# Keys and inputs of a recurrent head transposed as row tiles in one group, attention one weight tile earlier, and two multiplications on VectorE instead of GpSimd

## The reference, cut to what matters

```python
h = rmsnorm(x, w_norm_pre)
proj = h @ w_in                      # q_a k_a v_a z_a (attention), q_r f_r i_r z_r (recurrence)
# attention: 8 query heads, 2 key heads, chunks of 64 tokens; a chunk sees itself and the one before
s = q_a . k_a * 64 ** -0.5
p = softmax([s, sink])[..., :-1]     # one sink logit a head
o_a = (p @ v_a) * silu(z_a)
# recurrence: 4 heads of width 128
f = lb + (1 - lb) * sigmoid(f_r);  kk = 1 - f
G = cumsum(log f)                    # within a chunk
A = tril((q_r * exp(G)) @ (kk * exp(-G)).T)
o = A @ i_r + (q_r * exp(G)) @ S_prev      # S_prev: state carried from chunk to chunk
U = (kk * exp(G_last - G)).T @ i_r;  S = exp(G_last) * S_prev + U
o_r = rmsnorm(o, hgrn_norm) * silu(z_r)
y = [o_a, o_r] @ w_out
out = x + rmsnorm(y, w_norm_post)
```

## Time and profile before

| | |
|---|---|
| median of 3 runs | 909.15 us (907.79 to 909.39) |
| the profiled execution | 906.35 us |
| its span in the trace | 904.4 us |
| TensorE (PE) busy | 884.2 us, 98% |
| TensorE weight loads (PEld) busy | 725.4 us, 80% |
| VectorE (DVE) busy | 520.0 us, 58% |
| ScalarE (ACT) busy | 423.7 us, 47% |
| GpSimd (POOL) busy | 167.6 us, 19% |
| share of PE in the chain that ended last | 86% |
| granted TensorE clock, mean | 0.997 |

### The profile page before, as it was taken

One profiled execution on the slowest core, in us unless ns is written; L12 is line 12 of the kernel. 1 busy time (PEld: TensorE's weight loads), 2 busy tenths in 40 slices (PEclk: granted clock), 3 DMA queues, 4 the chain that ended last, 5 costly groups with the idle time before them and its releaser, 6 DMA issues.

```text
span 904.4 us, 12126 instructions
## 1 busy us (share of the span) xinstructions
PE 884.2 (98%) x4616; PEld 725.4 (80%) x4616; DVE 520.0 (58%) x829; ACT 423.7 (47%) x750; POOL 167.6 (19%) x122
## 2 busy tenths in 40 slices
PE   7998989989999999999999999999999999999997
PEld 6786867878888787888888878888888887888886
DVE  6758877675553765655244577555515366744523
ACT  7756365564355534544234444454423443445322
POOL 0001232430200023242020021353002001213102
PEclk9999999999999999999999999999999999999999
DMA  8686664747967842543676652444378553335463
GB/s 308 234 295 203 206 204 154 278 150 266 419 215 270 278 175 98 184 165 141 243 283 234 226 213 106 148 174 167 115 298 325 190 177 116 139 137 179 140 238 135
DMA packets 52633, 186.01 MB, mean 206 GB/s; under 512 B 5856, under 2 KB 6112, under 8 KB 52576
## 3 DMA queue, kind: packets, MB, share of 16 engines
q1 hardware_dynamic: 49840, 178.29, 55.5%
q10 hardware_dynamic: 2736, 6.95, 1.9%
HBM read 141.18 MB, written 44.04 MB: 205 GB/s over the span
## 4 chain that ended last, share of the span: by engine, by line
PE 86%; DVE 6%; issue 4%; ACT 2%; POOL 2%; DMA 1%; SPq 0%; DVEq 0%; ACTq 0%; POOLq 0%
PE bank L428 54%; PE bank L437 10%; PE turn_b L437 5%; PE score_b L437 5%; PE turn_b L476 2%; PE score_b L454 2%; PE bank L508 1%; PE bank L524 1%; PE bank L515 1%; PE bank L522 1%; PE bank L493 1%; DVE w_lo L865 1%; PE bank L501 1%; DMA w_raw<-in_weights 1%; PE turn_b L466 1%
## 5 line engine op out<-in xcount | busy, mean ns | idle before, releaser
L428 PE MATMUL bank<-h_hi,w_lo 128*128 128x512 f32 x832 | 329.2, 396 | 0.7 <-DVE w_lo L877 0.7
L428 PE MATMUL bank<-h_lo,w_hi 128*128 128x512 f32 x832 | 329.0, 395 | 0.0
L428 PE MATMUL bank<-h_hi,w_hi 128*128 128x512 f32 x832 | 327.5, 395 | 1.4 <-issue 0.6
L428 PEld LDWEIGHTS bank<-h_lo,w_hi 128*128 128x128 f32 x832 | 156.7, 188 | 36.7 <-issue 6.4
L428 PEld LDWEIGHTS bank<-h_hi,w_hi 128*128 128x128 f32 x832 | 156.7, 188 | 35.1 <-issue 2.7
L428 PEld LDWEIGHTS bank<-h_hi,w_lo 128*128 128x128 f32 x832 | 156.7, 188 | 33.8 <-DVE w_lo L877 1.4
L1135 POOL TENSOR_TENSOR probs<-probs,s_stats 128x1024 f32<-128x1024 f32 x16 | 33.1, 2067 | 349.6 <-DVE s_stats L1007 349.6
L865 DVE TENSOR_TENSOR w_lo<-w_raw,w_hi 128x1024 fp32r<-128x1024 f32 x37 | 47.2, 1282 | 33.0 <-ACT w_hi L656 33.0
L660 ACT ACTIVATE g_a<-g_b 128x512 f32<-128x512 f32 x32 | 20.2, 632 | 89.8 <-DVE g_b L929 89.8
L933 DVE SCALAR_TENSOR_TENSOR g_a<-g_b,g_a 128x512 f32<-128x512 f32 x32 | 35.3, 1102 | 44.2 <-ACT g_a L662 44.2
L1163 POOL TENSOR_TENSOR mix_lo<-v_r,mix_hi 128x512 fp32r<-128x512 f32 x16 | 20.7, 1294 | 169.9 <-ACT v_r L798 169.9
(11 more groups left out here) (161 smaller groups left out, 1439.6 us busy)
## 6 DMA issues: line engine op xcount, KB each, us to landing
w_hi<-kept_hi SPq DMA_DIRECT2D x96, 512.0 KB, 3.7
w_lo<-kept_lo SPq DMA_DIRECT2D x96, 512.0 KB, 4.7
w_raw<-in_weights SPq DMA_DIRECT2D x40, 512.0 KB, 5.5
kept_hi<-w_hi SPq DMA_DIRECT2D x34, 512.0 KB, 5.7
kept_lo<-w_lo SPq DMA_DIRECT2D x34, 512.0 KB, 7.2
x_in<-in_x_rows SPq DMA_DIRECT2D x8, 1024.0 KB, 7.2
x_in<-in_x SPq DMA_DIRECT2D x15, 512.0 KB, 6.8
out<-q_gate ACTq DMA_DIRECT2D x9, 512.0 KB, 9.4
```

The costliest lines, as they stand in the source:

```text
L428: mm = pe.matmul(acc(w)[:, :], stationary[:, s, k, :], moving[:, k, :], start=(m == 0), stop=(m == 3 * KT - 1), skip_group_check=True)
```

## The change

1. `SCORES0` goes from `Z0 + 3` to `Z0 + 2`: every quarter of attention is one weight tile earlier (scores at `w` = 8, 10, 12, 14). `weigh` moves from m = 17 to m = 20. The offsets of `MIXA` grow by one, so that those copies stay at steps 20 and 21.
2. `turn_keys` and `turn_inputs` go. `head_scores` (now `gate(h)`, m = 12) transposes both as 16 transposes of 64 partitions in two row groups, into the two banks of `score_b`; then, without waiting for a copy, it makes the scores in `head_b`. ScalarE copies both with one instruction of 128x1024 instead of two of 128x512. `head_states`, `scores(3)` and the start of the output projection wait for that copy (`kv_ready`).
3. `head_out` moves from m = 12 to m = 8, `head_sum` from m = 20 to m = 18, and it writes `score_b[:, 1, :]`. It no longer waits for `o_gated`; the scores of the next head do.
4. The normalisation of `probs` moves from GpSimd to the end of `softmax_sums` on VectorE, the product `k_mid` from GpSimd to VectorE, ahead of the scaling of `f_d`.

```diff
-SCORES0 = Z0 + 3
+SCORES0 = Z0 + 2
-MIXA = {SCORES0 + CHUNKS + 3: (0, 1), SCORES0 + CHUNKS + 4: (2, 3)}
+MIXA = {SCORES0 + CHUNKS + 4: (0, 1), SCORES0 + CHUNKS + 5: (2, 3)}
...
 # scores(t, q)
+                for h in range(HEADS):
+                    if gate(h) + 1 == SCORES0 + 2 * q:
+                        pe.wait_ge(kv_ready.sem, kv_ready.after(t, h))
...
-            def turn_keys(t, h):
+            def head_scores(t, h):
                 pe.wait_ge(k_mid_done.sem, k_mid_done.after(t, h))
+                pe.wait_ge(tile_read.sem, tile_read.after(t, value(h)))
+                pe.wait_ge(m_sub.sem, m_sub.after(t, PAIRS - 1 if gate(h) >= SCORES0 + CHUNKS else (gate(h) - SCORES0) // 2))
                 pe.wait_ge(o_rstd.sem, o_rstd.after(t, h - 1))
-                for p in range(PAIRS):
-                    mm = pe.transpose(head_b[:, pair(p)], k_mid[:, pair(p)], ident)
-                mm.then_inc(k_turned.sem, 1)
...
+                for a, src in enumerate((k_mid, v_r)):
+                    for p in range(PAIRS):
+                        for j in range(2):
+                            half = slice(64 * j, 64 * j + 64)
+                            mm = pe.transpose(score_b[:, j, chunk(PAIRS * a + p)], src[half, pair(p)], ident[half, half])
+                mm.then_inc(kv_turned.sem, 1)
+                pe.wait_ge(o_gated.sem, o_gated.after(t, h - 1))
                 for p in range(PAIRS):
                     mm = pe.matmul(head_b[:, pair(p)], k_mid[:, pair(p)], q_mid[:, pair(p)], start=True, stop=True)
                 mm.then_inc(a_done.sem, 1)
...
 # head_sum(t, h)
                 pe.wait_ge(o_low.sem, o_low.after(t, h))
-                pe.wait_ge(o_gated.sem, o_gated.after(t, h))
-                pe.matmul(head_b[:, :], ones_r[:, :], o_sq_hi, ...)
+                pe.matmul(score_b[:, 1, :], ones_r[:, :], o_sq_hi, ...)
...
 # between(t, w, m)
-                    if w == gate(h) and m == 4:
-                        turn_keys(t, h)
-                    if w == gate(h) and m == 10:
-                        turn_inputs(t, h)
-                    if w == gate(h) and m == 17:
+                    if w == gate(h) and m == 12:
                         head_scores(t, h)
-                    if w == gate(h) + 2 and m == 12:
+                    if w == gate(h) + 2 and m == 8:
                         head_out(t, h)
-                    if w == gate(h) + 3 and m == 20:
+                    if w == gate(h) + 3 and m == 18:
                         head_sum(t, h)
-                if m == 17 and not odd and 1 <= q <= PAIRS:
+                if m == 20 and not odd and 1 <= q <= PAIRS:
                     weigh(t, q - 1)
...
 # scalar, at s == gate(head), now behind the copy of turn_b
+                            act.wait_ge(kv_turned.sem, kv_turned.after(t, head))
+                            act.activation(kv_tok[:, :, :].rearrange("p a (b j n) -> p j (a b) n", j=2, n=CHUNK),
+                                           score_b[:, :, :].rearrange("p j (b n) -> p j b n", n=CHUNK), ACT.Copy).then_inc(kv_ready.sem, 1)
...
 # vector, softmax_sums(t, q)
-                dve.reciprocal(s_inv[:, :], s_sum[:, :]).then_inc(p_inv.sem, 1)
+                then(t, dve.reciprocal(s_inv[:, :], s_sum[:, :]))
+                dve.tensor_tensor(probs[:, :, :], probs[:, :, :], s_inv[:, :].unsqueeze(2).broadcast_to([P, 8, P]),
+                                  ALU.mult).then_inc(p_normed.sem, 1)
...
 # vector, kind 1 (step forget(h) + 2)
                         dve.wait_ge(f_exp.sem, f_exp.after(t, h_of))
+                        dve.wait_ge(a_done.sem, a_done.after(t, h_of - 1))
+                        dve.tensor_tensor(k_mid[:, :], f_a[:, :], f_b[:, :], ALU.mult).then_inc(k_mid_done.sem, 1)
                         dve.tensor_tensor(f_d[:, :], f_d[:, :], x_scale[:, :], ALU.mult).then_inc(f_d_scaled.sem, 1)
```

More of the change, by code:

```diff
@@ L234, in hybrid_block @@
         scored, turned, weighed = (count(n, PAIRS) for n in ("scored", "turned", "weighed"))
-        k_turned, v_turned, a_done, u_done = (count(n, HEADS) for n in ("k_turned", "v_turned", "a_done", "u_done"))
+        kv_turned, a_done, u_done = (count(n, HEADS) for n in ("kv_turned", "a_done", "u_done"))
         o_done, o_summed = count("o_done", HEADS), count("o_summed", HEADS)
@@ L241, in hybrid_block @@
         p_exp, p_turned, v_win_ready = count("p_exp", PAIRS), count("p_turned", PAIRS), count("v_win_ready", 1)
-        k_ready, v_ready, o_squared, o_rstd = (count(n, HEADS) for n in ("k_ready", "v_ready", "o_squared", "o_rstd"))
+        kv_ready, o_squared, o_rstd = (count(n, HEADS) for n in ("kv_ready", "o_squared", "o_rstd"))
         mixa_hi, mixh_hi = count("mixa_hi", QT), count("mixh_hi", HEADS)
@@ L252, in hybrid_block @@
         a_masked, state_done, o_gated, head_mixed = (count(n, HEADS) for n in ("a_masked", "state_done", "o_gated", "head_mixed"))
-        m_sub, p_inv, gated = (count(n, PAIRS) for n in ("m_sub", "p_inv", "gated"))
+        m_sub, gated = (count(n, PAIRS) for n in ("m_sub", "gated"))
         h_lo_done = count("h_lo_done", KT)
@@ L257, in hybrid_block @@
         y_read, y_biased, finished = count("y_read", 8), count("y_biased", 1), count("finished", 8 - len(Y_POOL))
-        dve_step = count("dve_step", 1 + len(ROPE_TILES) + PAIRS * 4 + HEADS * 8)
+        dve_step = count("dve_step", 1 + len(ROPE_TILES) + PAIRS * 5 + HEADS * 8)
         dve_setup, lb_step = sem("dve_setup"), sem("lb_step")
@@ L413, in _ @@
         def _(pe):
-            for c in (tile_done, x_summed, y_done, values_turned, scored, turned, weighed, k_turned, v_turned, a_done, u_done, o_done, o_summed):
+            for c in (tile_done, x_summed, y_done, values_turned, scored, turned, weighed, kv_turned, a_done, u_done, o_done, o_summed):
                 c.start(pe)
@@ L530, in head_sum @@
                 pe.wait_ge(o_low.sem, o_low.after(t, h))
-                pe.wait_ge(o_gated.sem, o_gated.after(t, h))
-                pe.matmul(head_b[:, :], ones_r[:, :], o_sq_hi, start=True, stop=False, skip_group_check=True)
-                pe.matmul(head_b[:, :], ones_r[:, :], o_sq_lo, start=False, stop=True,
+                pe.matmul(score_b[:, 1, :], ones_r[:, :], o_sq_hi, start=True, stop=False, skip_group_check=True)
+                pe.matmul(score_b[:, 1, :], ones_r[:, :], o_sq_lo, start=False, stop=True,
                           skip_group_check=True).then_inc(o_summed.sem, 1)
@@ L596, in _ @@
                 pe.wait_ge(mixa_lo.sem, mixa_lo.after(t, QT - 1))
+                pe.wait_ge(kv_ready.sem, kv_ready.after(t, HEADS - 1))
                 order = [(2 * w + i, b) for w in range(3) for b in range(4) for i in range(2)] + [(KT - 2, b) for b in range(4)]
@@ L635, in _ @@
         def _(act):
-            for c in (hi_split, swapped, gate_ln, gate_sig, f_ln, f_sig, f_log, f_exp, p_exp, p_turned, v_win_ready, k_ready, v_ready,
+            for c in (hi_split, swapped, gate_ln, gate_sig, f_ln, f_sig, f_log, f_exp, p_exp, p_turned, v_win_ready, kv_ready,
                       o_squared, o_rstd, mixa_hi, mixh_hi, x_squared, h_hi_done, y_squared, x_rstd, y_rstd, act_step):
@@ L759, in _ @@
                         gate_first(t, QT + h)
-                    for head in range(HEADS):
-                        if s == gate(head):
-                            act.wait_ge(k_turned.sem, k_turned.after(t, head))
-                            act.activation(kv_tok[:, 0, :], head_b[:, :], ACT.Copy).then_inc(k_ready.sem, 1)
                     if not odd and 1 <= q <= PAIRS:
@@ L800, in _ @@
                             act.wait_ge(o_summed.sem, o_summed.after(t, head))
-                            rstd(t, head_b[:, :], o_scale[:, :], P).then_inc(o_rstd.sem, 1)
+                            rstd(t, score_b[:, 1, :], o_scale[:, :], P).then_inc(o_rstd.sem, 1)
                     if s == V_TURN + 1:
@@ L1121, in _ @@
         def _(pool):
-            for c in (lo_split, k_mid_done, o_low, p_normed, mixa_lo, mixh_lo, x_added,
+            for c in (lo_split, o_low, mixa_lo, mixh_lo, x_added,
                       y_scaled, finished_pool):
@@ L1131, in split_lo @@
                 pool.tensor_tensor(w_lo[:, s, :, :], w_raw[:, i % RAW_SLOTS, :, :], w_hi[:, s, :, :], ALU.subtract).then_inc(lo_split.sem, 1)
-            def norm_probs(t, q):
-                pool.wait_ge(p_inv.sem, p_inv.after(t, q))
-                pool.tensor_tensor(probs[:, :, :], probs[:, :, :], s_inv[:, :].unsqueeze(2).broadcast_to([P, 8, P]),
-                                   ALU.mult).then_inc(p_normed.sem, 1)
             def add_x(tile, k):
@@ L1167, in _ @@
                                                ALU.subtract).then_inc(mixh_lo.sem, 1)
-                    if odd and 0 <= q < PAIRS:
-                        norm_probs(t, q)
                     for i in splits(t, s):
@@ L1172, in _ @@
                             split_lo(i)
-                    if kind == 1:
```

(3 more changed lines are left out.)

13 lines of the change are left out of this document (1 added, 12 removed).

## The result

The changed kernel takes 900.17 us, the median of four runs (899.35 to 901.49). The kernel before, timed beside it, takes 908.47 us, the median of four (906.3 to 909.39). The ratio is 0.9915, with a 95% interval of 0.9896 to 0.9934. The forecast was 900.8 us, in a range of 895.5 to 907.2.

A forecast was written before the change was run, and what follows sets the result against it. Matmul time was taken to bound token tiles 2 to 4, with VectorE's and ScalarE's pace also counting in the first. Gains of 6.9 + 1.5 = 8.4 us gave 900.8 us by the median, range 895.5 to 907.2.

The forecast's parts named there:

- The walk: First token tile, engine lists laid side by side: PE enters the output projection 6.9 us sooner; counting waits gave 5.7.
- The refund: First tile, VectorE: seven instructions stretched by GpSimd's two products give back 8 us together, against 7.2 added.
- The waits left: First tile, PE: waits remaining after the change sum to 6.5 us, against 11.7 lost before.
- the slack: `weigh(1)`: a wait of about 1.0 us in the first tile; 0.5 us to spare in token tiles 2 to 4.
- PE's own saving: Every tile: merged row-tiled transposes save 0.12 us a head, 0.5 a token tile, 2.0 over four.
- so 0.78 without them: PE: 16 row-tiled transposes cost 0.78 us, from 1.23 with four keys' transposes behind them.
- all waits of the first tile would go: Rival, first tile: 11.7 + 2.0 = 13.7 us gained, 895.5 us; chance 0.14.
- VectorE's pace would be no better: Rival, first tile: waits only change place, PE's own time alone is saved, 907.1 us; chance 0.16.
- the clock falls at the new wait: Rival, first tile: behind `head_scores(3)`'s wait of 2.8 us the slow clock takes 1.6 us, 902.4 us; chance 0.09.
- VectorE's list as the bound: Rival, first tile: the added 7.2 us come on VectorE's path without refund, 914.4 us; chance 0.09.
- no wait in token tiles 2 to 4: Later token tiles: PE still never waits, so 3 x 0.5 = 1.5 us gained.
- the loop: First tile, behind `v_r`: PE transposes, ScalarE copies and makes `mix_hi` and `w_hi`, then VectorE splits; a head still takes 29.8 us.

The follow-up runs named there:

- without part 4: Changed kernel with normalisation and `k_mid` back on GpSimd, all else as changed: 903.82 us, ratio 0.9954 to the kernel before.
- the split ahead of the copy: Changed kernel, with ScalarE making `w_hi` at gate steps ahead of its wait for the turned keys and values: 896.4 us, ratio 0.9875 to the kernel before.
- part 4 alone: Kernel before with only normalisation and `k_mid` moved from GpSimd to VectorE: 904.83 us, ratio 0.9964.
- two changes of order on ScalarE and GpSimd: Changed kernel with `w_hi` ahead of the wait for turned keys and values, and `MIXA`'s second pair at step 22 instead of 21: 894.63 us, ratio 0.9848.
- attention late: Changed kernel with attention back at its old weight tiles (scores at 9, 11, 13, 15), all else as changed: 910.74 us, ratio 1.0023 to the kernel before.
- Attention sooner alone: Kernel before with attention one weight tile sooner, `weigh` still at m = 17, both products on GpSimd: 907.73 us, ratio 0.9994.
- parts 1 and 4: Kernel before with attention one weight tile sooner, `weigh` at m = 17, and normalisation and `k_mid` on VectorE: 901.31 us, ratio 0.9929.
- with `head_sum` waiting: Changed kernel with `head_sum` waiting for `o_gated` again: 903.19 us, ratio 0.9939 to the kernel before.

## Why the prediction came out right, and where its sum was wrong

**The place.** PE's waits in the first token tile were to shrink, and they did. Idle time of PE there went from 10.1 to 4.4 us. `forget(2)` starts at 140.07; 139.5 was expected, and this profile began `w` = 8 some 1.3 us later than that of before, so on its clock it is 138.8. The walk's head of 29.8 us is 170.07 - 140.07 = 30.0 for head 2. Head 3 takes PE 30.0 us in the second profile.

**The refund.** L933 was to fall back from 2.14 to 0.69: L924 takes 0.68. The group's mean over 32 instructions is 720 ns after and 895 ns with the products back on GpSimd. The Trainium skill's rule in "SBUF — State Buffer", "Who interferes with whom", was cited for it. This case agrees twice: 0.68 us alone, 2.14 beside GpSimd, in the kernel before and again in the one without part 4. The 8 us of refund in the first tile are borne out as a whole: 150.69 us of VectorE's work became 149.68 with more than 7 added.

**The waits left.** Forecast, then measured from the starts on PE (the waits list shows a little less, as it counts only idle time): `weigh(0)` 0.5, measured 0.5; `weigh(1)` 1.0, none; `head_scores(2)` 1.7, about 1.1; `head_out(2)` 0.5, about 0.9; `head_scores(3)` 2.8, 1.9; `head_sum(2)` nothing, about 0.5. Sum 6.5, measured 4.9. Two small ones that the forecast didn't have, 0.4 at `head_states(1)` and 0.2 at `head_scores(0)`, bring it to 5.5, and in the first profile the slow clock behind `head_scores(3)` adds 1.1. The largest one stands where it was put and for its reason, as the split ahead of the copy shows. At `weigh(1)` the exponentials are ahead of the copy, as the walk had them, but the copy ends as PE comes to it: the slack is nil, where I had it at -1.0.
```profile
88.64 1.00 ACT L757 ACTIVATE probs_t<-turn_b 128x1024 f32<-128x1024 f32 x1
```
```profile
89.70 1.08 PE L479 MATMUL turn_b<-probs_t,v_win 128*64 128x256 f32 x8
```

**The term that was mis-sized.** PE's own saving was to be 0.5 us a tile and 2.0 in all; the tiles are 0.10 shorter, 0.4 in all, and 218.8 long, not 218.5. The failed step is "so 0.78 without them". I took 1.23 us for `turn(3)` with `turn_keys(1)` behind it, and subtracted the 0.45 that four full transposes cost between two products. But behind row tiles they don't cost that. The changed kernel has `turn(3)` without them:
```profile
341.76 0.39 PE L428 MATMUL bank<-h_hi,w_hi 128*128 128x512 f32 x1
342.08 0.71 PE L469 MATMUL turn_b<-sq_in,probs 64*128 64x64 f32 x16
342.72 0.50 PE L428 MATMUL bank<-h_hi,w_lo 128*128 128x512 f32 x1
343.06 0.40 PE L428 MATMUL bank<-h_lo,w_hi 128*128 128x512 f32 x1
```
That is 1.30 - 0.45 = 0.85 us, so the keys' transposes had cost 1.23 - 0.85 = 0.38. The row tiles have a price at the entry (0.32 us to the first one instead of 0.23) and one at the exit (0.34 between the first two products instead of 0.23), and groups in line can cost less than apart: `scores` costs 1.30 alone, `turn` 0.85, and both in line 1.79. With the keys at 0.38 the account closes to 0.05 us. Before, heads 2 and 3 paid 0.90 each, heads 0 and 1, whose keys stood behind a `turn`, 0.83 to 0.85. After, the merged group without its scores (0.91 us, as 1.36 - 0.45 in the kernel with part 4 alone) is 1.74 - 0.91 = 0.83 a head. So 3.5 - 3.3 = about 0.15 a tile, against 0.10 measured. `head_scores` and `weigh`, in one slot before and apart after, are no part of the difference: 2.12 us together, 0.90 and 1.22 apart.

The Trainium skill's rule in "TensorEngine Tiling (Array Packing)", "Key Properties", that a change of tiling mode drains the engine, was weighed with a second drain at the exit: 0.5 us in all. The measured 0.4 us is nearer to that reading than to mine, and the exit does show a second 0.11 us. But the exit was in the 1.23 us of the earlier trace rows as well. What I had too large was the price of the keys behind it, and that the two numbers agree is in part luck. That the 0.09 and the 0.11 are a drain isn't shown.

**What made up for it, and luck.** By the medians the gain is 8.3 us, by the means of two profiles 7.4. From `w` = 8 on, the two pairs of profiles give 5.77 and 8.45 us for the first tile, 7.1 on the mean, where 6.9 were forecast; the later tiles give 0.3 where 1.5 were. The prediction's own two counts of that tile, 6.9 by the walk and 5.7 by the waits, were 1.2 us apart, and these profiles don't decide between them. So the profiles give 7.4 us in all, and the median's 8.3 comes nearer the forecast of 8.4 than the parts of the sum do: that is partly luck. The clock alone moves the first tile by 1.1 to 1.6 us between executions of one kernel, and its start by 1.8 to 1.9.

**The rivals.** That all waits of the first tile would go was wrong: one of 1.84 us stays. With two changes of order on ScalarE and GpSimd it came true, 894.63 against the 895.5 worked out for it. That VectorE's pace would be no better was wrong up to `forget(2)` and right for head 2, which keeps 30.0 us. That the clock falls at the new wait is half true, in one of two profiles and for some 1.1 us. VectorE's list as the bound is excluded by part 4 alone, which gains 3.6 us. No rival of mine said what the kernel with attention late shows: a shared buffer turns an edit that is free in one schedule into a wait in each tile in another. The step "no wait in token tiles 2 to 4" held because attention had moved.

## What to carry to other kernels

A change of order is a set of places that hold each other. Attention sooner alone gains nothing here (0.9994), and all the rest with attention late loses (1.0023), while attention sooner with the two products on VectorE gains 6.6 us and all the parts together 8.3: find for each edit the buffer or slot that another must free. In a queue that runs in order, work that waits for nothing belongs ahead of work that waits; moving the splits of the gate steps past a copy gained 3.8 us, half as much as the whole change, and the prediction had named the loop without asking whether its order was needed. When a cost is read by subtraction from a group, take the subtrahend from the same neighbourhood.

## What the runs showed of the hardware

A wait on PE is not priced by its length alone. In the first token tile the products behind some waits ran 0.43 us apart, at the lower level of 1.2 GHz (granted clock 0.50), and behind others of the same length they didn't. Behind the 1.84 us at `head_scores(3)` two or three products are slow in the changed kernel's first profile and none in its second. Behind waits of 2.6 us none are slow in the kernels with part 4 alone and with parts 1 and 4, five in the one with attention sooner alone, and in the two profiles of the kernel before seven or three behind `weigh(0)` and none behind `head_sum`. Behind 2.83 us, with `head_sum` waiting, there are twelve, 2.4 us on top. In the second profile of the kernel before, five are slow behind two waits of only 1.3 and 1.4 us that stand close together. The kernel with the fewest waits also has the narrowest times, 0.5 us from lowest to highest over four runs, where the kernel before has 4.5 over 17 in the same sitting; four runs are few.

What sets whether and for how long the clock falls behind such a wait is open: no run was made for it.
